# Two down projections that read the activations' columns in permuted orders

## What is computed

```python
def swiglu(h, w_gate, w_up, w_down):
    return (jax.nn.silu(h @ w_gate) * (h @ w_up)) @ w_down

for layer in range(DEPTH):          # DEPTH = 2
    ...
    h = rms_norm(x, ffn_pre_g[layer])
    f = swiglu(h, ffn_w_gate[layer], ffn_w_up[layer], ffn_w_down[layer])
    x = x + rms_norm(f, ffn_post_g[layer])
```

## Time and profile before

| | us |
|---|---|
| median of 3 runs | 982.19 |
| lowest, highest | 981.73, 982.43 |
| span of the profiled execution, first to last instruction | 980.3 |

### The profile page before, as it was taken

How to read it: one execution, slowest core, us unless ns; L and a number is a source line. 1 busy time by engine, 2 the same in 40 slices (tenths; PEclk the granted TensorE clock), 3 DMA queues, 4 the chain that set the end, 5 groups by cost and what they waited for, 6 DMA issues and landing times.

```text
span 980.3 us, 18888 instructions
## 1 busy us (share of the span) xinstructions
PE 958.4 (98%) x7971; PEld 923.9 (94%) x7971; DVE 720.6 (74%) x1340; ACT 542.4 (55%) x837; POOL 25.4 (3%) x54
## 2 busy tenths in 40 slices
PE   8999999999999999999999999999999999999997
PEld 8889999999998988899999997998999999999996
DVE  7965897777658777698879788555654879888653
ACT  7554664454447366565444545456755567666542
POOL 0300000000000000000000000000220000000000
PEclk9999999999999999999999999999999999999999
DMA  8536376766744734368767882653343545555621
GB/s 298 190 116 238 128 266 255 255 251 225 295 172 168 266 129 140 116 212 304 265 251 267 331 315 76 245 185 116 111 149 132 199 157 207 181 203 184 216 87 43
DMA packets 27588, 194.72 MB, mean 199 GB/s; under 512 B 3056, under 2 KB 3184, under 8 KB 4592
## 3 DMA queue, kind: packets, MB, share of 16 engines
q1 hardware_dynamic: 27504, 193.51, 54.7%
HBM read 192.45 MB, written 1.05 MB: 197 GB/s over the span
## 4 chain that ended last, share of the span: by engine, by line
PE 89%; ACT 4%; DVE 4%; issue 2%; DMA 1%; POOL 0%; SPq 0%; DVEq 0%; ACTq 0%
PE bank L508 25%; PE bank L509 24%; PE bank L514 23%; PE bank L639 2%; PE bank L665 2%; PE bank L569 2%; PE bank L563 2%; ACT s_whi L906 2%; PE bank L564 2%; PE bank L528 2%; PE bank L535 1%; PE bank L529 1%; PE bank L649 1%; DVE s_wlo L1382 1%; DMA s_xT<-in_xT 1%
## 5 line engine op out<-in xcount | busy, mean ns | idle before, releaser
L1382 DVE TENSOR_TENSOR s_wlo<-s_raw,s_whi 128x512 fp32r<-128x512 f32 (+1 forms) x364 | 372.3, 1065 | 138.1 <-ACT s_whi L906 137.9
L906 ACT ACTIVATE s_whi<-s_raw 128x1024 fp32r<-128x1024 f32 (+2 forms) x233 | 304.8, 1335 | 215.6 <-PE bank L514 205.9
L508 PE MATMUL bank<-s_hh,s_whi 128*128 128x256 f32 x1400 | 393.6, 281 | 1.1 <-DVE s_wlo L1382 0.7
L509 PE MATMUL bank<-s_hl,s_whi 128*128 128x256 f32 x1400 | 387.6, 277 | 0.0
L514 PE MATMUL bank<-s_hh,s_wlo 128*128 128x256 f32 x1383 | 382.8, 277 | 0.0
L508 PEld LDWEIGHTS bank<-s_hh,s_whi 128*128 128x128 f32 x1400 | 263.3, 188 | 6.9 <-issue 5.9
L509 PEld LDWEIGHTS bank<-s_hl,s_whi 128*128 128x128 f32 x1400 | 263.2, 188 | 0.1
L514 PEld LDWEIGHTS bank<-s_hh,s_wlo 128*128 128x128 f32 x1383 | 259.8, 188 | 0.0
L508 PE MATMUL bank<-s_ph,s_whi 128*128 128x256 f32 x528 | 146.4, 277 | 0.0
L509 PE MATMUL bank<-s_pl,s_whi 128*128 128x256 f32 x528 | 145.8, 276 | 0.0
L514 PE MATMUL bank<-s_ph,s_wlo 128*128 128x256 f32 x516 | 142.5, 276 | 0.0
(11 more groups left out here) (238 smaller groups left out, 1285.3 us busy)
## 6 DMA issues: line engine op xcount, KB each, us to landing
s_raw<-in_gu SPq DMA_DIRECT2D x44, 1024.0 KB, 4.9
s_raw<-in_dn SPq DMA_DIRECT2D x33, 1024.0 KB, 4.9
s_raw<-in_wada SPq DMA_DIRECT2D x24, 1024.0 KB, 5.7
s_raw<-in_up SPq DMA_DIRECT2D x22, 1024.0 KB, 4.9
s_raw<-in_wo SPq DMA_DIRECT2D x8, 1024.0 KB, 4.9
s_raw<-in_win_g SPq DMA_DIRECT2D x8, 1024.0 KB, 4.9
s_raw<-in_mla SPq DMA_DIRECT2D x4, 1024.0 KB, 5.4
s_raw<-in_wkv_v SPq DMA_DIRECT2D x4, 1024.0 KB, 4.9
```

The lines of the kernel that those rows point to most:

```text
L508: e.matmul(out, hi, xh[:, k, :], start=first, stop=False, skip_group_check=True)
L509: e.matmul(out, hi, xl[:, k, :], start=False, stop=False, skip_group_check=True)
L906: e.activation(whi[w % SPLIT][:, at], raw[p % RAW][:, at], ACT.Copy).then_inc(S.hi.tick((w, c0)), 1)
L1382: e.tensor_tensor(wlo[s][:, at], raw[p % RAW][:, at], whi[s][:, at].bitcast(F32), ALU.subtract).then_inc(S.lo.tick((i, j), (i, "all")), 1)
```

## The change

The table `LINES` gives every output tile of `dn0` and of `dn1` an order of its 256 columns as (ways, width, apart). Columns go in blocks of `width`. With `apart` false the 256 columns are cut into `ways` equal parts, and one block is taken from each part by turns. With `apart` true blocks are dealt out to `ways` hands, and all blocks of the first hand are read (every `ways`-th block), then all of the second. Output tiles 0 and 1 share an order. The moving operand (`s_ph` or `s_pl`) and the output in PSUM are given the same order, so every token's column lands where it did. Nothing else about the data moves: same bytes, same tiles, same weight loads.

`product` does this in a branch of its own, which leaves before `halves` is looked at. So in `dn0` and `dn1` the pieces of 128 columns are gone, and there are 8 matmuls fewer in all. `dn2` and all other projections are as before.

```diff
+LINES = {"dn0": {0: (2, 16, True), 2: (2, 16, False), 3: (2, 32, False), 4: (2, 64, False), 5: (2, 32, True), 6: (4, 16, False), 7: (2, 8, False)},
+         "dn1": {0: (4, 16, True), 2: (2, 8, True), 3: (2, 4, False), 4: (2, 4, True), 5: (8, 16, False), 6: (4, 32, False), 7: (2, 64, True)}}
...
-            def product(name, t, out, xh, xl, k, first, last, event=None, halves=False):
+            def lines(ap, name, n):
+
+                n = 0 if n == 1 else n
+                if n not in LINES.get(name, {}):
+                    return ap
+                ways, width, apart = LINES[name][n]
+                if apart:
+                    return ap.rearrange("p (a b c) -> p b a c", b=ways, c=width)
+                return ap.rearrange("p (b a c) -> p a b c", b=ways, c=width)
+
+            def product(name, t, out, xh, xl, k, first, last, event=None, halves=False, n=None):
 
                 hi, lo, used = weight(name, t)
+                if name in LINES:
+                    out = lines(out, name, n)
+                    e.matmul(out, hi, lines(xh[:, k, :], name, n), start=first, stop=False, skip_group_check=True)
+                    e.matmul(out, hi, lines(xl[:, k, :], name, n), start=False, stop=False, skip_group_check=True)
+                    m = e.matmul(out, lo, lines(xh[:, k, :], name, n), start=False, stop=last, skip_group_check=True)
+                    if used is not None or event is not None:
+                        m.then_inc(S.gemm.tick(("used", used), event), 1)
+                    return
```

More of the change, by code:

```diff
@@ L552, in tiles @@
                         product(name, (n + j) * nk + k, outs[j], xh, xl, k, k == 0, k == nk - 1,
-                                event if k == nk - 1 else None, name in HALVED and j == 0 and k == 1 and n % HALVED[name] == 0)
+                                event if k == nk - 1 else None, name in HALVED and j == 0 and k == 1 and n % HALVED[name] == 0,
+                                n + j)
             def token_block(name, g, nk, xh, xl, k, tb):
@@ L761, in lead_dn @@
                                 k == 0 and j == 0, k == NF - 1, (name, 0) if k == NF - 1 and j == 1 else None,
-                                k == 1 and j == 0)
+                                k == 1 and j == 0, j)
             feed_forward(0, "h1", sqb[3])
```

## The result

| | us |
|---|---|
| before, median of 4 runs | 982.31 |
| changed, median of 4 runs (lowest, highest) | 989.15 (988.37, 989.79) |
| ratio, 95% interval | 1.0066 (1.0052 to 1.0079) |
| span of the profiled execution, changed | 987.3 |

The change makes the kernel 0.66% slower, some 5 to 8 us. The forecast was 981.2 us and the range ended at 989.0, so both the value and the range were missed.

What follows compares the result with a forecast made beforehand. The prediction took PE's number of matmuls times their distance to bound both projections. Removing pairs gave -1.02 us and the order zero: 982.19 - 1.02 = 981.2 us, called same, with range 979.0 to 989.0.

Steps and rivals of the forecast that it cites:

- The pairs, -1.02 us: In dn0 and dn1, eight matmuls run as two pieces, four per projection; dropping them saves 0.127 us each.
- The fast pace: In dn0 and dn1, plain matmuls start 0.1134 us apart; the forecast took this to hold without pairs, loss nothing.
- I take zero: Cost forecast for all 1056 matmuls of dn0 and dn1 reading SBUF and writing PSUM in blocks: none.
- the prediction's own mark: Test in dn0 and dn1: the forecast is wrong if any tile with blocks is over 2 ns from 113.4.
- The turn of one weight load per matmul is the limit: In dn0 and dn1, weight loads set the 113.4 ns distance; the stream of columns fits under, with little to spare.
- cover, about 2 ns: In dn0 and dn1, some 2 ns of extra stream time per matmul would be hidden under the weight load.
- The slower pace: Rival: dn0 and dn1 fall to the 117.7 ns seen in gu0; +3.5 us net, 985.7 us, chance 0.20.
- The price by block: Rival: each block start in dn0 and dn1 costs one cycle; +7.1 - 1.0 = +6.1, 988.3 us, chance 0.19.
- tile by tile mark: In dn0 and dn1, narrow tiles slow, wide ones not: 27 ns for 64 blocks, 1.7 ns for 4.
- The strict rule: Rival: non-contiguous PSUM output slows every dn0 and dn1 tile alike, up to 1088 us; chance 0.05.
- a gain that rested on nothing but starts read to 0.01 us: Rival: in dn0 and dn1 the distance falls to 111.5 ns; -3.0 us, 979.2 us, chance 0.10.
- a rival's point: The lower price by block for dn0 and dn1, 988.3 us, taken into the range as its slow case.

Runs made afterwards that it cites:

- the natural run: Changed kernel with all reading orders taken out and the pairs left out too: ratio 0.9988 to the kernel before, 982.4 against 983.4 us.

## Why the prediction failed, and where it held

- **The pairs, -1.02 us.** Right. Each stretch fell by 0.506 us when only they were taken out, from 60.353 to 59.847.
- **The fast pace isn't lost for want of pairs.** Right: the natural run holds 113.3 through all 1056 matmuls.
- **"I take zero" for the order.** This is the step that failed. It measured +6.9 us. The argument was that the stream of columns is the same, so it costs the same. It looked at the moving read alone. Its time depends on where the next weights are read from at the same time, and at the place of this kernel every order tried that changes the sequence of addresses modulo 256 bytes was slower. By the prediction's own mark, 2 ns from 113.4, 15 of the 16 output tiles miss.
- **"The turn of one weight load per matmul is the limit" at the fast pace.** Too strong. The earlier trace rows show that a shorter stream isn't faster, and they still do. But I took from them that the stream has cover, about 2 ns. The slower pace was the sign against it, and I left it without a cause: same instructions, shapes and clock, 4.4 ns more. It was the right row and I priced it as a rival instead of asking what differs.
- **The slower pace as a rival, +3.5 us.** It took part: tile 7 of `dn1` is at 117.8 because the tile ahead left it so, 0.3 us. As a size for all tiles it was too small, since 117.8 is the slow pace of the natural order and most orders have their own, 119 to 127.
- **The price by block, +6.1 us net.** Its sum is near the measured net 5.9, by chance. It had 64 blocks 25 ns above and 4 blocks free, and (2, 4, True) with 64 blocks is 4.5 above, (4, 32, False) with 8 blocks 6.6. Its tile by tile mark is what tells it from the truth.
- **PSUM.** The strict rule of the Trainium skill ("PSUM — Partial Sum Buffer", Specifications (TRN2)) had a chance of 0.05. No block down to 8 bytes in PSUM costs anything here, so it doesn't hold for these matmuls. I called "Advanced Engine Details and Errata", Memory Cachelines, milder; in fact that section of the Trainium skill holds the strict sentence on PSUM as well. For SBUF the same section gives lines of 16 bytes, at full performance as long as accesses that follow each other hit one line. That isn't enough to call an order free: every read here has at least four neighbouring columns, 16 bytes, and orders cost up to 20 ns all the same.
- **The range.** It ended at 989.0 and the median is 989.15. I gave 0.10 to a gain that rested on nothing but starts read to 0.01 us, and ended the range at a round value just above a rival's point, when that rival's own size was a guess by a factor of two.

## What to carry to other kernels

When TensorE runs matmuls back to back with a weight load each, look at the distance between starts, not at busy time, and compare it between stretches of the same shape. If two stretches differ by some ns, look at the SBUF addresses of moving operand and weights relative to each other (here modulo 256 bytes, -64 was best) and at what stands ahead of the stretch. Here a reading order in blocks of 256 bytes was free when it was entered at the fast pace, and so was an output in PSUM in pieces of 8 bytes.

## What the runs showed of the hardware

- Matmuls of 256 columns with 128 columns of weights go at 113.3 to 133.3 ns by nothing but the addresses, the order of the moving read and what ran ahead, with the granted clock at its upper level (1.00 in these stretches).
- The time from one matmul to the next depends on the difference of the two addresses: with both moved by 64 bytes, 14 orders gave their old numbers to 0.2 ns, and 256 bytes more on the activations alone left 113.3 as it was.
- The natural order has two steady paces at one and the same place, 113.3 and 117.8 ns. A different order ahead of it is enough to change from one to the other, and one matmul in two pieces of 128 columns changes back.
- Reading each 64 bytes with its parts in reverse costs 20 ns a matmul, whether in halves or quarters. This has no explanation here.
- Why the free distance is free, and how the two reads meet inside the chip, isn't shown.
